# A decoder layer on one core: first output rows transposed ten units later, exps ahead of crossings, pairs 4 to 7 merged on GpSimd

## The chip, the cores and the metric

The kernel runs on one core of one Trainium2 chip. The metric is device time in microseconds (us) of one execution, the median of several runs. Engines: PE is TensorE, PEld its weight loads, DVE VectorE, ACT ScalarE, POOL GpSimd, SP the queue that issues most transfers.

## The reference

One layer for 512 tokens of width 1024, all in float32. One projection `h = x @ w_in` feeds two attention branches of 8 heads each, whose outputs are gated, joined, projected and normalised:

```python
o_a = _dsa_branch(qa, ka, va, iq, ik, iw) * jax.nn.silu(ga)      # A: top-128 keys of an indexer
o_b = _mla_branch(c_q, c_kv, k_rope, ...) * jax.nn.silu(gb)      # B: latent attention, 96-wide q and k
out = jnp.concatenate([o_a, o_b], axis=-1) @ w_out[l]
x = _layernorm(DEEPNORM_ALPHA * x + out, ln_g[l], ln_b[l])
```

Both branches are causal softmax attention, `p = softmax(masked scores * scale)`, `o = p @ v`. Branch A masks all keys but those that its indexer chose.

## The kernel before

**Stages.** Until about 170 us the kernel multiplies x with w_in and makes queries, keys and values. Matrices that need full precision are split into a high and a low part, and a product is three matmuls (high by high, high by low, low by high). Then comes attention, and beside it and behind it the output projection with `w_out` and the layer norm.

**Units.** Attention is a sequence of `NU` = 64 units, one for each (branch, block of 128 query tokens, head). Units 0 to 31 are branch A, units 32 to 63 branch B. The four token tiles come in the order 3, 2, 1, 0, eight heads each, so a unit has 512, 384, 256 and then 128 keys, in each branch. Each engine has its own loop over the unit number u, written out by hand, and semaphores join them:

- PE, iteration u (L1355): `scores(u)`, then the transposes of unit u-2 (`T_LAG`), then the product with v of unit u-4 (`outputs`), then what is put beside: `o_transposes(i, b)` (tile i's gated output rows, half b: 0 for branch A, 1 for B) and some steps of `out_products` (the output projection).
- DVE, iteration u (L992): `mask_unit(u)` adds the mask and finds the maximum, `probs_low(u-2)` (branch B only) makes the low part of the transposed probabilities, and then, in the units that the tables name, the normalising and gating of a tile, `copy_oT_lo`, `gate_obT`, `read_pair`, `merge_pair` and the pieces of the layer norm.
- ACT, iteration u (L665): `copy_probsT(u-2)`, then `copy_oT_hi` and `cross_pair` where due, then `exp_unit(u)`.

The scores of u wait for the mask of u-2, the mask of u for the transposes of u-4, the transposes of u for its exp, the product for the copies.

**PSUM banks of the transposes.** Two banks take all transposes in turn, those of the units and of the output rows. The table `slots` (L82) is their order, and `slot(n)` (L1257) lets a transpose wait until the one two places ahead was read: a unit of branch A by its copy, one of B by `probs_low`, output rows by `copy_oT_lo` or `gate_obT`. `O_FIRST` = 22 puts tile 0's branch A rows behind unit 22's transposes, which PE issues in iteration `O_FIRST + T_LAG` = 24; ACT and DVE read them in their iterations 24.

**Output projection.** The first half of tile 0's 48 steps starts at iteration `A_HALF_AT` = 34, two steps an iteration for 12 iterations. The second half is at iterations 49 to 54, four an iteration, and needs `copy_oT_lo(0, 1)`. From iteration 55 on tile 1 follows with six an iteration.

**Pairs.** In branch B the products of two heads form a pair; pairs 0 to 15, four for each tile. For pair g, DVE's `read_pair(g)` at iteration 38 + 2g sums parts out of PSUM, ACT's `cross_pair(g)` one iteration later moves halves across partitions with two copies, and `merge_pair(g)` adds them with two instructions (L295). Pairs below `POOL_PAIRS` = 8 are merged by DVE in iteration 39 + 2g, behind its own mask and `probs_low`; the rest by POOL in a loop of its own (L468), in which the square roots of the layer norm (`root`) and `scale_gate(2)`, `scale_gate(3)` have fixed places. The second instruction of a pair's merge on POOL waits for nothing on DVE. `gate_obT(i)` waits for all four pairs of tile i.

**Vb.** In ACT's iterations 32 and 33 `vb_high(1)` to `vb_high(3)` (three 512-wide copies, L654) stand behind the exp.

The places that the change and the steps below touch are O_FIRST, A_HALF_AT and POOL_PAIRS (L1395 to L1397), ACT's loop and POOL's loop over pairs.

Of the kernel before, what the change touches and what calls it, by code (L numbers as in the profile page):

```python
# [27 lines left out]
def build(nc, x, xT, positions, freqs, w_in, q_norm_g, w_uq, kv_norm_g, w_ukv, w_out, ln_g, ln_b, out):  # L28
# [40 lines left out]
    NU = 2 * NU_A  # L69
# [3 lines left out]
    def unit(u):  # L73
        v, h = divmod(u, HEADS)
        m = ORDER[v % TT]
        return v, m, h, (m + 1) * P


    O_AFTER = [[NU_A + HEADS * (i + 1) + OT_AT - T_LAG + b for b in range(2)] for i in range(TT - 1)] + [[NU, NU]]
    O_AFTER[0][0] = O_FIRST  # L80
    slots = []
# [109 lines left out]
    with ExitStack() as ctx:  # L191
# [83 lines left out]
        def wait_tok(eng, g, m):  # L275

            eng.wait_ge(acc_read[m], 2 * (g + 1))
# [10 lines left out]
        def merge_pair(eng, g):  # L288

            eng.wait_ge(pair_crossed, 2 * (g + 1))  # L290
            if g % 4 == 0 and g > 0:
                eng.wait_ge(oT_lo_ready, 2 * (g // 4))
            for a in range(2):
                rows = slice(V_DIM * a, V_DIM * (a + 1))
                eng.tensor_tensor(obT[rows, g % 4], half_sum[rows, g % 2, a], crossed[rows, g % 2],  # L295
                                  ALU.add).then_inc(pair_merged, 1)
                if g >= POOL_PAIRS:
                    eng.wait_ge(pair_merged, 2 * g + a + 1)
# [69 lines left out]
        def _(pool):  # L368
# [58 lines left out]
            def scale_gate(i):  # L427

                m = ORDER[i]
                pool.wait_ge(rinv_ready, i + 1)  # L430
                wait_tok(pool, G_GB, m)
                g3 = gate[:, m, A_WIDTH:].rearrange("p (h d) -> p h d", h=HEADS)
                pool.tensor_tensor(g3, g3, rinv.unsqueeze(2).broadcast_to([P, HEADS, V_DIM]), ALU.mult).then_inc(gate_scaled, 1)
# [27 lines left out]
            def root(i):  # L461

                pool.wait_ge(var_ready, i + 1)
                pool.tensor_tensor(rstd, aggr[:, 2:3], minus_half[:, 0:1], ALU.pow).then_inc(rstd_ready, 1)


            scale_gate(1)
            for g in range(POOL_PAIRS, NPAIR):  # L468
                merge_pair(pool, g)
                if g == 9:  # L470
                    root(0)
                if g == 10:
                    scale_gate(2)
                if g == NPAIR - 3:
                    scale_gate(3)
                    root(1)
# [5 lines left out]
        def _(act):  # L482
# [115 lines left out]
            def evac_qpeT(j):  # L598

                quad, r = divmod(j, 2)  # L600
                act.wait_ge(acc_ready, A_END + quad + 1)
                ins = act.activation(qbT[NOPE:B_QK, 4 * quad + r, :], ps_y[32 * r:32 * r + 32, quad], ACT.Copy)
                if r == 1:
                    ins.then_inc(acc_read[2 + quad], 1)


            def exp_unit(u):
                N = unit(u)[3]
                act.wait_ge(masked_ready, u + 1)
                act.activation(probs[:, u % NPROBS, 0:N], probs[:, u % NPROBS, 0:N], ACT.Exp, bias=neg_max[:, u % 8:u % 8 + 1],  # L610
                               scale=-1.0, accum_out=row_sum[:, u:u + 1]).then_inc(probs_ready, 1)
# [12 lines left out]
            def copy_probsT(u):  # L624
                N = unit(u)[3]
                act.wait_ge(transposed, slot_of[u] + 1)
                if u >= 3:
                    act.wait_ge(pv_done, u - 2)
                dst = probsT[:, u % 3, 0:N] if u < NU_A else probsT_b[:, u % 3, 0, 0:N]
                act.activation(dst, ps_pT[:, slot_of[u] % 2, 0:N], ACT.Copy).then_inc(probsT_copied, 1)  # L630

            def copy_oT_hi(i, b):
                n = slot_of[i, b]
                if i == 0 and b == 0:
                    act.wait_ge(wo_hi_ready, 2 * KT)
                if i >= 2 and b == 0:
                    act.wait_ge(out_ps_ready, 2 * (i - 1))
                if b == 0:
                    act.wait_ge(transposed, n + 1)
                    src = ps_pT[:, n % 2].rearrange("p (a b) -> p a b", a=4)  # L640
                else:
                    act.wait_ge(obT_ready, i + 1)
                    src = obT[:, :, :]
                act.activation((oT0, oT1)[i % 2][:, 0, 4 * b:4 * b + 4, :], src, ACT.Copy).then_inc(oT_hi_ready, 1)  # L644

            def vb_high(n):

                j = VB_ORDER[n]
                if n == 1:
                    act.wait_ge(scores_ready, NU_A)  # L650
                    act.wait_ge(masked_ready, NU_A)
                if j == 2:
                    act.wait_ge(vb_lo_dve, 2)
                act.activation(vb_parts[j][:, :, 0:4:3], vb[:, j, :].rearrange("p (q a d) -> p q a d", a=2, d=V_DIM),  # L654
                               ACT.Copy).then_inc(vb_hi_ready, 1)

            def cross_pair(g):

                act.wait_ge(pair_read, g + 1)
                if g >= 2:  # L660
                    act.wait_ge(pair_merged, 2 * (g - 1))
                act.activation(crossed[0:V_DIM, g % 2], half_sum[V_DIM:P, g % 2, 0], ACT.Copy).then_inc(pair_crossed, 1)
                act.activation(crossed[V_DIM:P, g % 2], half_sum[0:V_DIM, g % 2, 1], ACT.Copy).then_inc(pair_crossed, 1)

            for u in range(NU + T_LAG):  # L665
                if u >= T_LAG:
                    copy_probsT(u - T_LAG)
                i, j = divmod(u - NU_A, HEADS)
                if u == O_FIRST + T_LAG:
                    copy_oT_hi(0, 0)  # L670
                if 1 < i < TT and j == OT_AT:
                    copy_oT_hi(i - 1, 0)
                if 0 < i < TT and j == OT_AT + 2:
                    copy_oT_hi(i - 1, 1)
                g = PAIR_AT.get(u - 1)
                if g is not None:
                    cross_pair(g)
                if 2 <= u < NU:
                    exp_unit(u)
                if 0 <= u - PET_AT - 1 < 4:  # L680
                    evac_qpeT(u - PET_AT - 1)
                if u == PET_AT + 7:
                    act.wait_ge(acc_ready, A_END + 3)
                    act.activation(kbT[NOPE:B_QK, 0, :], ps_y[0:ROPE_D, 0], ACT.Copy).then_inc(acc_read[2], 2)
                if u == VB_EARLY:
                    vb_high(0)
                if u == NU_A:
                    vb_high(1)
                    vb_high(2)
                if u == NU_A + 1:  # L690
                    vb_high(3)
# [7 lines left out]
        def _(dve):  # L699
# [160 lines left out]
            def evac_qpeT(j):  # L860

                quad, r = divmod(j, 2)
                dve.wait_ge(acc_ready, A_END + quad + 1)
                ins = V.tensor_copy(qbT[NOPE:B_QK, 4 * quad + 2 + r, :], ps_y[64 + 32 * r:96 + 32 * r, quad])
                if r == 1:
                    ins.then_inc(acc_read[2 + quad], 1)
# [40 lines left out]
            def copy_oT_lo(i, b):  # L907
                dst = (oT0, oT1)[i % 2]
                dve.wait_ge(oT_hi_ready, 2 * i + b + 1)
                src = ps_pT[:, slot_of[i, b] % 2].rearrange("p (a b) -> p a b", a=4) if b == 0 else obT[:, :, :]  # L910
                V.tensor_tensor(dst[:, 1, 4 * b:4 * b + 4, :], src, dst[:, 0, 4 * b:4 * b + 4, :],  # L911
                                ALU.subtract).then_inc(oT_lo_ready, 1)
# [79 lines left out]
            for u in range(NU):  # L992
# [15 lines left out]
                if 0 <= u - PET_AT - 1 < 4:  # L1008
                    evac_qpeT(u - PET_AT - 1)
                if u == O_FIRST + T_LAG:  # L1010
                    copy_oT_lo(0, 0)
# [6 lines left out]
                if u in PAIR_AT:  # L1018
                    read_pair(PAIR_AT[u])
                if u - 1 in PAIR_AT and PAIR_AT[u - 1] < POOL_PAIRS:  # L1020
                    merge_pair(V, PAIR_AT[u - 1])
# [31 lines left out]
        def _(pe):  # L1053
# [301 lines left out]
            for u in range(NU + PV_LAG):  # L1355
# [10 lines left out]
                i, j = divmod(u - NU_A, HEADS)  # L1366
                if u == O_FIRST + T_LAG:
                    o_transposes(0, 0)
                if 0 < i < TT and OT_AT <= j < OT_AT + 2 and (i > 1 or j > OT_AT):
                    o_transposes(i - 1, j - OT_AT)  # L1370
                if 0 <= u - A_HALF_AT < 12:
                    out_products(0, 2 * (u - A_HALF_AT), 2 * (u - A_HALF_AT + 1))
                if 0 <= u - OUT_AT[0] - 2 < 6:
# [18 lines left out]
QT_AT, KT_AT = 4, 4  # L1392
PET_AT = 8
WO_ORDER = (1, 2, 3, 4, 5, 6, 7, 0)
O_FIRST = 22  # L1395
A_HALF_AT = 34
POOL_PAIRS = 8  # L1397
VB_EARLY = 20
Q_ROTATE_AT = [28, 33, 38, 43]

# [38 lines left out]
```

## Time and profile before

| | |
|---|---|
| median of 3 runs | 308.17 us (307.63 to 308.52) |
| profiled execution | 307.56 us |
| its span, first to last instruction | 305.7 us |
| mean granted TensorE clock | 0.993 of full speed |
| PE busy | 293.8 us (96%) |
| DVE, ACT, POOL busy | 236.8, 171.5, 159.8 us |
| chain of work that ended last | 92% on PE |

Times inside the trace count from the first instruction. A matmul's end is modelled and lies a little behind the start of the next one, so a PE delay is best read from starts. In brackets behind a row stands the idle time before it and who ended it.

### The profile page before, as it was taken

The numbers are of one execution on the slowest core, as the hardware profiler recorded it, in microseconds if no ns is written. First come the engines' busy times: TensorE is split into PE (matmuls) and PEld (weight loads), VectorE is DVE, ScalarE is ACT, GpSimd is POOL, SyncE is SP. The second block draws the span as 40 slices with busy tenths as digits, with TensorE's granted clock in tenths as the row PEclk, the third lists the DMA queues.
The fourth block names the chain that finished last, engine by engine and source line by source line (L and its number), as shares of the span: only waits on it lengthen the run. The fifth ranks groups of instructions, "written<-read, shape, count | busy, mean of one in ns | idle before, by whom it ended". The sixth has DMA issues, their size and how long they took to land.

```text
span 305.7 us, 5164 instructions
## 1 busy us (share of the span) xinstructions
PE 293.8 (96%) x1646; PEld 253.2 (83%) x1646; DVE 236.8 (77%) x540; ACT 171.5 (56%) x411; POOL 159.8 (52%) x180
## 2 busy tenths in 40 slices
PE   7999999999999999999999999999999999999990
PEld 6999988888888888888888789997677787888890
DVE  1999968879999999994134645755789998887785
ACT  5844355684152262383277887997967885464200
POOL 4898954305999965435317696820491010335211
PEclk9999999999999999999999999999999999999997
DMA  7974542200533723220068234131940000040411
GB/s 251 343 198 132 151 142 69 69 2 0 146 95 106 207 69 89 85 69 2 0 154 232 99 138 159 49 62 28 360 165 0 2 0 3 0 138 2 137 69 69
DMA packets 14777, 31.24 MB, mean 102 GB/s; under 512 B 1728, under 2 KB 4288, under 8 KB 14752
## 3 DMA queue, kind: packets, MB, share of 16 engines
q1 hardware_dynamic: 14192, 30.60, 32.3%
q10 hardware_dynamic: 560, 0.33, 0.4%
q8 instruction: 13, 0.21, 0.3%
q14 instruction: 12, 0.10, 0.1%
HBM read 26.28 MB, written 2.10 MB: 93 GB/s over the span
## 4 chain that ended last, share of the span: by engine, by line
PE 92%; DVE 2%; DMA 2%; ACT 1%; issue 1%; DVEq 0%; SPq 0%; ACTq 0%
PE ps L1059 49%; PE ps L1348 14%; PE ps L1275 6%; PE ps L1225 5%; PE ps L1291 5%; PE ps L1306 3%; PE ps L1216 2%; DMA x_raw<-in_xT 2%; PE ps L1219 2%; PE ps L1131 1%; PE ps L1069 1%; PE ps L1150 1%; PE ps L1320 1%; PE ps L1121 1%; ACT oT L644 1%
## 5 line engine op out<-in xcount | busy, mean ns | idle before, releaser
L403 POOL TENSOR_TENSOR w_lo<-w_raw,w_hi 128x512 fp32r<-128x512 f32 (+3 forms) x62 | 80.1, 1313 | 37.6 <-ACT w_hi L496 37.6
L1059 PE MATMUL ps<-w_hi,x_lo 128*128 128x512 f32 (+2 forms) x224 | 82.4, 371 | 0.0
L1059 PE MATMUL ps<-w_lo,x_hi 128*128 128x512 f32 (+2 forms) x224 | 82.4, 371 | 0.0
L496 ACT ACTIVATE w_hi<-w_raw 128x512 fp32r<-128x512 f32 (+3 forms) x62 | 36.3, 591 | 73.3 <-PE ps L1059 72.4
L1059 PE MATMUL ps<-w_hi,x_hi 128*128 128x512 f32 (+1 forms) x192 | 74.5, 388 | 0.0
L1059 PEld LDWEIGHTS ps<-w_hi,x_lo 128*128 128x128 f32 x224 | 42.1, 188 | 6.5
L1059 PEld LDWEIGHTS ps<-w_lo,x_hi 128*128 128x128 f32 x224 | 42.1, 188 | 5.8
L1348 PE MATMUL ps<-wo_hi,oT 128*128 128x512 f32 (+1 forms) x144 | 44.3, 372 | 0.0
L610 ACT ACTIVATE probs<-probs,small 128x512 f32<-128x512 f32 (+3 forms) x64 | 35.7, 558 | 10.9 <-DVE small L879 10.5
L1059 PEld LDWEIGHTS ps<-w_hi,x_hi 128*128 128x128 f32 x192 | 36.0, 188 | 5.9
L1275 PE MATMUL ps<-ident,probs 128*128 128x128 f32 x160 | 28.3, 274 | 1.9 <-ACT probs L610 0.9
L1275 PEld LDWEIGHTS ps<-ident,probs 128*128 128x128 f32 x160 | 20.1, 140 | 11.3 <-issue 6.3
L1348 PEld LDWEIGHTS ps<-wo_hi,oT 128*128 128x128 f32 x144 | 25.7, 189 | 3.3
L832 DVE MATCH_REPLACE8 score<-small,score 128x256 f32<-128x256 f32 (+2 forms) x48 | 25.6, 544 | 0.0
L879 DVE CUSTOM_DVE_ANT_0 probs<-ps,score 128x512 f32<-128x512 f32 (+2 forms) x24 | 13.3, 556 | 14.7 <-PE ps L1219 14.7
L829 DVE MAX8 small<-score 128x8 f32<-128x256 f32 (+2 forms) x48 | 23.5, 547 | 0.0
L1225 PE MATMUL ps<-kbT,qbT 96*128 96x512 f32 (+3 forms) x64 | 22.7, 435 | 0.0
L295 POOL TENSOR_TENSOR obT<-half_sum,crossed 64x128 f32<-64x128 f32 x16 | 8.8, 550 | 24.5 <-DVE oT L911 13.7
L1291 PE MATMUL ps<-va,probsT 128*128 128x64 f32 x160 | 21.4, 264 | 0.0
L1291 PEld LDWEIGHTS ps<-va,probsT 128*128 128x128 f32 x160 | 20.6, 193 | 0.6 <-issue 0.6
L879 DVE CUSTOM_DVE_ANT_0 probs<-ps,causal 128x128 f32<-128x128 f32 (+3 forms) x40 | 17.6, 444 | 3.5 <-PE ps L1225 1.6
L630 ACT ACTIVATE probsT_b<-ps 128x512 fp32r<-128x512 f32 (+3 forms) x32 | 13.8, 431 | 8.2 <-PE ps L1275 8.1
(164 smaller groups left out, 565.0 us busy)
## 6 DMA issues: line engine op xcount, KB each, us to landing
w_raw<-in_w_in SPq DMA_DIRECT2D x20, 512.0 KB, 3.6
kaT_swap<-kaT SPq DMA_DIRECT2D x8, 256.0 KB, 3.7
w_raw<-in_w_out SPq DMA_DIRECT2D x4, 512.0 KB, 5.1
wo_early<-in_w_out SPq DMA_DIRECT2D x4, 512.0 KB, 4.1
wo_raw_b<-in_w_out SPq DMA_DIRECT2D x4, 512.0 KB, 5.4
x_res<-in_x SPq DMA_DIRECT2D x4, 512.0 KB, 7.0
w_raw<-in_w_in SPq DMA_DIRECT2D x4, 416.0 KB, 3.9
x_raw<-in_xT SPq DMA_DIRECT2D x3, 512.0 KB, 6.4
```

The source lines that it names most:

```text
L403: pool.tensor_tensor(w_lo[:, s, 0:n], w_raw[:, s, 0:n], w_hi[:, s, 0:n], ALU.subtract).then_inc(w_lo_ready, 1)
L496: act.activation(dst, w_raw[:, s, 0:n], ACT.Copy).then_inc(w_hi_ready, 1)
L610: act.activation(probs[:, u % NPROBS, 0:N], probs[:, u % NPROBS, 0:N], ACT.Exp, bias=neg_max[:, u % 8:u % 8 + 1], scale=-1.0, accum_out=ro ...
L630: act.activation(dst, ps_pT[:, slot_of[u] % 2, 0:N], ACT.Copy).then_inc(probsT_copied, 1)
L829: step(V.max(top8[:, 8 * j:8 * j + 8], sc))
L832: step(V.match_replace(out=sc, in_to_replace=top8[:, 8 * j:8 * j + 8], in_values=sc, imm_value=TAKEN))
L879: V.tensor_tensor_reduce(out=probs[:, u % NPROBS, 0:N], in0=ps_s[:, u % 2, 0:N], in1=bias, scale=-scale, scalar=3.0e38, op0=ALU.add, op1=A ...
L1059: ins = mm(dst, a, b, start=start and j == 0, stop=stop and j == len(pairs) - 1)
L1225: ins = mm(ps_s[:, b, 0:N], qbT[:, h, t], kbT[:, h, 0:N], start=True, stop=True)
L1275: ins = nc.tensor.transpose(bank[:, j * P:(j + 1) * P], probs[:, u % NPROBS, j * P:(j + 1) * P], ident[:, :])
L1291: ins = mm(ps_o[:, v % 2, h * A_DIM:(h + 1) * A_DIM], probsT[:, u % 3, j * P:(j + 1) * P], va[:, j, h * A_DIM:(h + 1) * A_DIM], start=(j = ...
L1348: ins = mm(out_ps(i, b), oT[i % 2][:, o, k, :], w[:, wcols], start=(r == 0), stop=(r == 3 * KT - 1))
```

## The change

Five numbers and places change. Tile 0's branch A output rows are transposed ten units later (iteration 34, behind unit 32's transposes), and the first half of its output projection starts at iteration 36. DVE merges pairs 0 to 3 only, POOL 4 to 15, and `scale_gate(1)` moves behind two of POOL's new merges. In ACT's iteration the exp comes ahead of `copy_oT_hi(i - 1, 1)` and of `cross_pair`, but stays behind `copy_probsT` and behind `copy_oT_hi(.., 0)`. All of the work stays the same.

```diff
-            scale_gate(1)
             for g in range(POOL_PAIRS, NPAIR):
+                if g == POOL_PAIRS + 2:
+                    scale_gate(1)
                 merge_pair(pool, g)
...
                     copy_oT_hi(0, 0)
                 if 1 < i < TT and j == OT_AT:
                     copy_oT_hi(i - 1, 0)
+                if 2 <= u < NU:
+                    exp_unit(u)
                 if 0 < i < TT and j == OT_AT + 2:
                     copy_oT_hi(i - 1, 1)
                 g = PAIR_AT.get(u - 1)
                 if g is not None:
                     cross_pair(g)
-                if 2 <= u < NU:
-                    exp_unit(u)
...
-O_FIRST = 22
-A_HALF_AT = 34
-POOL_PAIRS = 8
+O_FIRST = 32
+A_HALF_AT = 36
+POOL_PAIRS = 4
```

ACT, iterations 39 and 40 of before (copy, crossing of pair 0, exp, then copy and exp):

```order
L630 ACTIVATE probsT_b_92<-ps 128x512 [waits pv_done,transposed]
L662 ACTIVATE crossed_110<-half_sum_103 64x128 [waits pair_read]
L663 ACTIVATE crossed_110<-half_sum_103 64x128
L610 ACTIVATE probs_97,small_107<-probs_97,small_107 128x512 [waits masked_ready]
L630 ACTIVATE probsT_b_92<-ps 128x512 [waits pv_done,transposed]
L610 ACTIVATE probs_97,small_107<-probs_97,small_107 128x384 [waits masked_ready]
```

The same iterations of the changed kernel, whose lines count one more:

```order
L631 ACTIVATE probsT_b_92<-ps 128x512 [waits pv_done,transposed]
L611 ACTIVATE probs_97,small_107<-probs_97,small_107 128x512 [waits masked_ready]
L663 ACTIVATE crossed_110<-half_sum_103 64x128 [waits pair_read]
L664 ACTIVATE crossed_110<-half_sum_103 64x128
L631 ACTIVATE probsT_b_92<-ps 128x512 [waits pv_done,transposed]
L611 ACTIVATE probs_97,small_107<-probs_97,small_107 128x384 [waits masked_ready]
```

The crossing now stands behind an instruction that waits for DVE's mask of the same unit.

ACT, iterations 33 to 35 of the changed kernel, with the copy of tile 0's output rows (oT_66) between unit 32's copy and unit 34's exp:

```order
L631 ACTIVATE probsT<-ps 128x128 [waits pv_done,transposed]
L611 ACTIVATE probs,small<-probs,small 128x512 [waits masked_ready]
L655 ACTIVATE vb_parts_95<-vb 128x4x2x64 [waits vb_lo_dve]
L631 ACTIVATE probsT_b<-ps 128x512 [waits pv_done,transposed]
L645 ACTIVATE oT_66<-ps 128x512 [waits transposed,wo_hi_ready]
L611 ACTIVATE probs,small<-probs,small 128x512 [waits masked_ready]
L631 ACTIVATE probsT_b<-ps 128x512 [waits pv_done,transposed]
```

Before, that copy stood ahead of unit 24's exp. The copy of unit 32 is the first of branch B, and it is behind the last of the vb copies in both kernels.

## Rows read from the trace of the kernel before

**Rows 1.** The page: the span, and the chain that ended last, by engine.

```profile
span 305.7 us, 5164 instructions
...
PE 92%; DVE 2%; DMA 2%; ACT 1%; issue 1%; DVEq 0%; SPq 0%; ACTq 0%
```

**Rows 2.** Timeline, PE and PEld, iterations 24 to 26: start, length, engine, line, what.

```profile
206.32 0.61 PE L1320 MATMUL ps<-ident,gate 128*128 128x128 f32 x4
206.68 0.31 PE L1216 MATMUL ps<-kaT,qaT 128*128 128x128 f32 x1
...
208.40 0.14 PEld L1275 LDWEIGHTS ps<-ident,probs 128*128 128x128 f32 x1 [0.58 <-DVE oT L911]
```

**Rows 3.** Timeline, iterations 34 and 35: PE, then ACT's and DVE's copies of unit 32.

```profile
214.95 1.08 PE L1225 MATMUL ps<-kbT,qbT 96*128 96x512 f32 x2
215.86 0.60 PE L1275 MATMUL ps<-ident,probs 128*128 128x128 f32 x4
...
216.44 0.48 PE L1348 MATMUL ps<-wo_hi,oT 128*128 128x512 f32 x1
...
217.64 0.58 ACT L630 ACTIVATE probsT_b<-ps 128x512 fp32r<-128x512 f32 x1
...
218.25 0.69 DVE L919 TENSOR_TENSOR probsT_b<-ps,probsT_b 128x512 fp32r<-128x512 f32 x1 [0.58 <-ACT probsT_b L630]
```

**Rows 4.** Timeline, iterations 39 to 47: masks, exp, crossing and transposes.

```profile
226.79 0.68 DVE L879 CUSTOM_DVE_ANT_0 probs<-ps,causal 128x512 f32<-128x512 f32 x1
...
233.40 0.56 DVE L879 CUSTOM_DVE_ANT_0 probs<-ps,causal 128x384 f32<-128x384 f32 x1
...
234.00 0.62 ACT L610 ACTIVATE probs<-probs,small 128x384 f32<-128x384 f32 x1 [0.35 <-DVE small L879]
...
235.01 0.55 DVE L879 CUSTOM_DVE_ANT_0 probs<-ps,causal 128x384 f32<-128x384 f32 x1
...
239.31 0.31 ACT L662 ACTIVATE crossed<-half_sum 64x128 f32<-64x128 f32 x1
...
240.62 0.56 DVE L879 CUSTOM_DVE_ANT_0 probs<-ps,causal 128x384 f32<-128x384 f32 x1
...
241.72 0.36 PEld L1275 LDWEIGHTS ps<-ident,probs 128*128 128x128 f32 x3 [0.35 <-DVE probsT_b L919]
```

**Rows 5.** Timeline, PE, iteration 49: scores of unit 49, transposes of unit 47.

```profile
243.63 0.60 PE L1225 MATMUL ps<-kbT,qbT 96*128 96x256 f32 x2
244.90 0.52 PE L1275 MATMUL ps<-ident,probs 128*128 128x128 f32 x3 [0.68 <-ACT probs L610]
```

**Rows 6.** Timeline, iterations 53 and 55: DVE's merge of pair 7, and PE.

```profile
255.03 0.60 DVE L295 TENSOR_TENSOR obT<-half_sum,crossed 64x128 f32<-64x128 f32 x2
...
256.72 0.60 PE L1225 MATMUL ps<-kbT,qbT 96*128 96x256 f32 x2
257.81 0.44 PE L1275 MATMUL ps<-ident,probs 128*128 128x128 f32 x2 [0.49 <-DVE probsT_b L919]
```

**Rows 7.** Timeline, iterations 55 to 60, by engine: DVE, ACT, POOL and PE.

```profile
258.87 0.41 DVE L879 CUSTOM_DVE_ANT_0 probs<-ps,causal 128x256 f32<-128x256 f32 x1
259.54 0.68 DVE L911 TENSOR_TENSOR oT<-obT,oT 128x512 fp32r<-128x512 f32 x1
...
262.84 0.31 ACT L662 ACTIVATE crossed<-half_sum 64x128 f32<-64x128 f32 x1
263.89 0.40 ACT L610 ACTIVATE probs<-probs,small 128x128 f32<-128x128 f32 x1 [0.41 <-DVE small L879]
...
263.63 1.54 POOL L295 TENSOR_TENSOR obT<-half_sum,crossed 64x128 f32<-64x128 f32 x2 [2.26 <-ACT crossed L663]
268.49 1.00 POOL L295 TENSOR_TENSOR obT<-half_sum,crossed 64x128 f32<-64x128 f32 x2 [2.69 <-ACT crossed L663]
...
266.90 0.40 ACT L610 ACTIVATE probs<-probs,small 128x128 f32<-128x128 f32 x1 [2.22 <-DVE small L879]
...
268.00 0.27 PE L1275 MATMUL ps<-ident,probs 128*128 128x128 f32 x1
```

## The prediction

> **What bounds the kernel now.** First the page: the chain that ended last lies 92% on PE, of a span of 305.7 us [rows 1]. So only two things move the end: PE's work, which this change leaves as it is, and the moments in which PE waits. I then looked at who PE waits for and at the timeline of the 64 attention units. From unit 56 on PE runs without a gap until it is done, so a wait saved or added among the units goes to the end one for one. In branch B and the end of branch A there are three waits that the change aims at.
>
> - Iteration 26: 0.58 us [rows 2] until DVE has read the output rows out of the bank that unit 24's transposes need; by starts it is 0.60.
> - Iteration 49: the scores of a 256-key unit take 0.45 (half of the 0.91 between the two starts of the 512-key unit in [rows 3]). The transposes could start at 243.63 + 0.45 = 244.08 and start at 244.90 [rows 5]: 0.82, for unit 47's exp, which stands behind the output copy and the crossing on ACT.
> - Iteration 55: 256.72 + 0.45 = 257.17 against 257.81 [rows 6]: 0.64, for DVE's `probs_low`, which is late.
>
> Together 2.06 us. A fourth, around iterations 30 and 31, comes from normalising and gating on DVE and stays.
>
> **The change part by part.** I go along PE's time and call "shift" how much later than before an iteration starts, with work that was moved counted where it now stands.
>
> *Output rows out of iteration 24.* The four transposes take 206.68 - 206.32 = 0.36 [rows 2], the wait 0.60. Iteration 34 starts 0.96 early, at 213.99 instead of 214.95 [rows 3]. ACT and DVE there are chained to PE and move along.
>
> *Output rows into iteration 34.* The new slot order is 32, rows, 33, 34. So unit 33's transposes take the bank of unit 32 and need `probs_low(32)`, which before only unit 34's needed, an iteration later. ACT reaches unit 32's copy behind three vb copies: 217.64 before, now 216.68. `probs_low(32)` starts 0.61 later [rows 3], at 217.29, and releases PE at its end, 0.69 + 0.06 later: 218.04. And PE? Scores 0.91 and then 0.58 up to the place where the projection steps stood (216.44 - 215.86) bring it to 215.48; a short wait of 0.06 for unit 31's copy, the rows' transposes 0.36, and iteration 35 starts at 215.90, its scores end at 216.81. It has no projection steps any more (two of them took 0.55 in each of iterations 34 and 35, the distance from 216.44 to the next scores). **PE waits 1.23 us in iteration 35.** Shift after it: -0.96 + 0.36 + 0.06 + 0.05 + 1.23 - 2 x 0.55 = about -0.37. The four steps come back in iterations 46 and 47.
>
> ACT's copy of the rows and DVE's `copy_oT_lo(0, 0)` fit: 0.6 each, while PE stands.
>
> *Exp ahead of the crossing, while DVE still merges.* This is the step to watch. In iteration 39 + 2g DVE runs mask, `probs_low`, merge; the merge waits for the crossing, and the crossing now waits for the exp, which waits for the mask that DVE has just made. The round for a 384-key unit: mask to exp 234.00 - 233.40 = 0.60, exp 0.62, crossing's start to the mask behind the merge 240.62 - 239.31 = 1.31 [rows 4]. So 2.53 us from an odd mask to the next, with DVE idle for part of it. The even iteration takes 235.01 - 233.40 = 1.61 [rows 4]. A pair of units costs DVE 4.14 us. The masks of before, which kept PE's pace, took 240.62 - 226.79 = 13.83 for seven units, of which a good part was the first, longest ones and a merge that took 1.5 us; units 43 to 46 went at 3.7 a pair. DVE becomes the pace. From mask 39 at 226.79 - 0.37 = 226.42: iteration 39, 512 keys, 2.94 (0.1 more for the mask, 0.1 for the exp and 0.2 for unit 37's copy ahead of it); then 1.6, 2.5, 1.6, 2.5, 1.6, 2.5, in all 12.4, for masks 40 to 46: mask 46 at about 241.79 instead of 240.62. From that mask to the weight load of unit 45's transposes it took 241.72 - 240.62 = 1.10, and there the load waited for `probs_low` already [rows 4]: no slack was left. Now it loads at 242.89. PE took these transposes 0.11 behind the load, at 241.83; now it is 0.37 early but has two projection steps more in iteration 46, 0.46, and would be there at 241.92. **PE waits 1.0 us in iteration 47.**
>
> *Iteration 49.* The 0.82 is gone: exp 47 now starts 0.60 behind its mask. But the output copy `copy_oT_hi(0, 1)` is behind it, 0.62 later, and the projection's second half needs `copy_oT_lo(0, 1)` in iteration 49. Mask 47 comes 2.16 behind mask 46 (`probs_low`, gate and `read_pair` lie between), at 243.95; + 0.60 + 0.62 + 0.65 for exp and high part, + 0.73 for the low part: ready at 246.55. PE, freed at 242.92, has 3.4 us of matmuls to do until then, 246.33: **0.2 us.**
>
> *Merges 4 to 7 off DVE.* 0.60 each [rows 6]. Three of them were hidden; pair 7's stood ahead of the layer norm pieces and mask 54, and without it `probs_low(52)` is in time: the 0.64 of iteration 55 is gone. On POOL, mostly idle there, a pair takes 1.00 [rows 7]; `gate_obT(1)` needs pair 7 some 0.5 us after it is ready. `scale_gate(1)`, 1.0 behind pair 5, has ten units of room. Each costs nothing.
>
> *Iterations 55 to 60.* A chain ran here with 0.46 to spare: exp 58 started at 266.90, its transposes can follow 0.64 later, and PE took them at 268.00 [rows 7]. Exp 58 waits for mask 58, that for `ln_scale(0, 0)`, that for POOL's `root(0)`, that for pair 9's merge and so for its crossing. In the frame of before: PE is 0.64 earlier, and so is DVE's chain (0.60 to 0.64, the merge). Added are: `copy_oT_hi(1, 1)` behind exp 55, which starts 0.45 behind mask 55 at 258.87 and takes 0.51, so the low part starts at 258.87 + 0.45 + 0.51 + 0.65 = 260.48 instead of 259.54, +0.94 [rows 7]; the crossing of pair 9 behind exp 57, at 263.89 + 0.40 = 264.29 instead of 262.84, +1.45; and pair 9's merge takes 1.00 instead of 1.54, if nothing disturbs it, -0.54. In sum +1.85 on a slack of 0.46: **PE waits 1.4 us in iteration 60** (1.35 with the smaller roundings). Later places have over 1 us in hand.
>
> The sum: 1.23 + 1.0 + 0.2 + 1.35 = 3.8 added, 2.06 removed, **+1.7 us**. Against the profiled execution's 307.56 that is 309.3. The three runs have a median of 308.17, 0.6 above it; I put the sum on the median: 309.9.
>
> **A rule that bears on it.** Pair 9's merge on POOL took 1.54 us, others 1.00 [rows 7], and DVE ran a layer norm piece with two SBUF inputs beside it. The Trainium skill (SBUF — State Buffer, "Who interferes with whom") says that a DVE instruction with two SBUF inputs and a GpSimd instruction that reads SBUF lock each other out for a whole instruction. By that rule, the trace agrees, and more merges on POOL are more chances for it. As a mechanism here: if the merge of pair 9 meets `ln_centre` again it takes 1.54, not 1.00, the wait in iteration 60 is 1.9 and the sum +2.2: 310.4. I take 1.00, since in my timeline `ln_centre` is over when the crossing ends.
>
> **Rivals.**
>
> - *Faster: DVE does not fall behind.* One mechanism: the round over ACT is hidden, because the first units of the stretch are long and DVE has more in hand than I count. Then there is no wait in iteration 47 and none in 60, and what is left is 1.2 - 2.06 = -0.8: 307.3; should unit 32's copy come in time too, -2.1: 306.1. It decides at mask 46: before 240.9 there is no loss. For it speaks that DVE is idle in part of each odd iteration; against it that the load behind mask 46 had no slack before.
> - *About the same.* Only one of the two late waits is there in full; for example the layer norm chain fits because crossing 9 is not held up: 1.23 + 1.0 + 0.2 - 2.06 = +0.4: 308.5.
> - *The lock* above: 310.4.
> - *The change is not what it says:* "ahead of its copies" does not hold for `copy_probsT`, which still precedes the exp. If the exp did gain on unit copies, nothing above would change, since exps of units 34 to 46 are paced by masks.
>
> **How the numbers follow.** A measurement of this kernel tells a change from none at about 0.3%, 0.9 us. My forecast 309.9 gets 0.48, the lock 0.10, the middle case 0.24, the faster rival 0.18. Slower by over 0.3% is the first two, 0.58; same 0.24; faster 0.18. The unknown parts are the three waits, each the small difference of two long chains, good to 0.4 us each. The range takes the middle case, the near end of the faster one and the lock with 0.6 on top: 307.2 to 311.0.
>
> **What would show it.** No wait before unit 24 to 27's transposes; a wait of over 1 us before unit 33's transposes, ended by DVE's `probs_low`; DVE's merges of pairs 0 to 3 each with some 0.8 us of idle time before them, ended by ACT's crossing; a wait before unit 45's transposes; none before 53's; pair 9's crossing behind exp 57 and a wait before unit 58's transposes, ended by ACT's exp. I am wrong if masks 40 to 46 keep PE's pace, or if PE's waits in the units together are no longer than before.

## The result, and the profile after

The changed kernel takes **311.63 us** (median of 4 runs, 311.33 to 311.75) against 307.93 for the kernel before on the same chip; the ratio is 1.0116, 95% interval 1.0098 to 1.0135. It is 3.7 us slower. Slower was right, but I had said 309.9 and at most 311.0: less than half of the loss was in my sum. The profiled execution took 311.70, with a span of 309.9 against 305.7 [rows 1]. Executions of one and the same kernel can come out some 1.7 us apart by what happens in their first 15 us (of `p_best` below: 306.01 to 306.64 and 307.80 to 308.17), so small differences between the kernels below are read from waits and distances and not from medians.

The page after: the span, and the chain that ended last, which lies less on PE and more on DVE and ACT.

```profile
span 309.9 us, 5166 instructions
...
PE 85%; DVE 5%; issue 3%; ACT 2%; DMA 2%; POOL 0%; SPq 0%; DVEq 0%; ACTq 0%; POOLq 0%
```

The waits of PE after, by who ended them: line and what it waited for, then us in total, times, longest. The first line below is the start of the program, the others are attention and the steps behind it.

```profile
PE ps L1070 <- ACT w_hi L497: 2.3, 3, 1.2
PE ps L1276 <- DVE probsT_b L920: 1.9, 2, 1.0
...
PE ps L1226 <- DVE small L880: 0.9, 1, 0.9
PE ps L1321 <- DVE probsT_b L920: 0.5, 1, 0.5
PE ps L1349 <- issue: 0.3, 1, 0.3
```

Where PE stands, from its timeline (start, length, engine, line, what, idle time before it and who ended it):

```profile
218.35 0.66 PE L1276 MATMUL ps<-ident,probs 128*128 128x128 f32 x4 [1.00 <-DVE probsT_b L920]
...
240.39 0.60 PE L1307 MATMUL ps<-probsT_b,vb_parts 128*128 128x256 f32 x3
241.10 0.66 PE L1321 MATMUL ps<-ident,gate 128*128 128x128 f32 x4
...
243.74 0.55 PE L1276 MATMUL ps<-ident,probs 128*128 128x128 f32 x3 [0.88 <-DVE probsT_b L920]
...
247.45 0.47 PE L1349 MATMUL ps<-wo_hi,oT 128*128 128x512 f32 x1
...
270.12 0.49 PE L1226 MATMUL ps<-kbT,qbT 96*128 96x128 f32 x2 [0.93 <-DVE small L880]
270.74 0.30 PE L1276 MATMUL ps<-ident,probs 128*128 128x128 f32 x1
...
273.68 0.66 PE L1321 MATMUL ps<-ident,gate 128*128 128x128 f32 x4 [0.47 <-DVE probsT_b L920]
...
291.38 0.47 PE L1349 MATMUL ps<-wo_hi,oT 128*128 128x512 f32 x1 [0.31 <-issue]
```

By distances between starts, each against the same pair of instructions where nothing waits, these cost:

| place | forecast | measured |
|---|---|---|
| iteration 35, transposes of unit 33 | 1.23 | 1.18 |
| iteration 46, tile 0's branch B rows | none | **0.27** |
| iteration 47, transposes of unit 45 | 1.0 | 1.05 |
| iteration 49, projection's second half | 0.2 | 0.3 |
| iteration 60, scores of 60 and transposes of 58 | 1.35 | 1.08 + 0.40 |
| iteration 61, tile 2's branch A rows | none | **0.63** |
| first projection step of tile 3 | none | **0.44** |
| iterations 26, 49 and 55 of before, gone | -2.06 | -2.06 |

For iteration 46 the pair is the product and the rows' transposes: 241.10 - 240.39 = 0.71 against 0.44 in the kernel before. The measured terms make 5.35 - 2.06 = 3.3. From the start of iteration 24 to PE's last matmul it takes 302.57 - 205.82 = 96.75 us instead of 298.35 - 205.43 = 92.92, so 3.83 more. The other 0.5 lies right behind the waits, where the next matmuls follow more slowly: the whole stretches that hold the waits of iterations 46, 47, 60, 61 and of tile 3 are 0.32, 1.10, 1.73, 0.68 and 0.57 us longer than in `a_noexp` below, which has none of these waits, and so each 0.05 to 0.25 longer than the wait in it. The last 0.4 of the span's 4.2 lies ahead of iteration 24 (205.82 against 205.43), where the two kernels do the same; other executions differ there too. I use this **distance** for the experiments, since it leaves the start out.

DVE's round in the stretch of pairs 1 to 3, from DVE's timeline: mask 43, merge, mask 44, mask 45, merge, mask 46.

```profile
235.84 0.55 DVE L880 CUSTOM_DVE_ANT_0 probs<-ps,causal 128x384 f32<-128x384 f32 x1
...
237.84 0.60 DVE L295 TENSOR_TENSOR obT<-half_sum,crossed 64x128 f32<-64x128 f32 x2 [0.97 <-ACT crossed L664]
238.47 0.56 DVE L880 CUSTOM_DVE_ANT_0 probs<-ps,causal 128x384 f32<-128x384 f32 x1
...
240.02 0.55 DVE L880 CUSTOM_DVE_ANT_0 probs<-ps,causal 128x384 f32<-128x384 f32 x1
...
242.02 0.60 DVE L295 TENSOR_TENSOR obT<-half_sum,crossed 64x128 f32<-64x128 f32 x2 [0.97 <-ACT crossed L664]
242.65 0.56 DVE L880 CUSTOM_DVE_ANT_0 probs<-ps,causal 128x384 f32<-128x384 f32 x1
```

An odd round takes 238.47 - 235.84 = 2.63, an even one 240.02 - 238.47 = 1.55. DVE stands idle for 0.97 us with the next mask ready to be made (PE had started the scores of 44 at 235.90), because a merge is ahead of it in its queue. ACT's part of the same round, exp 43 and the crossing of pair 2:

```profile
236.43 0.62 ACT L611 ACTIVATE probs<-probs,small 128x384 f32<-128x384 f32 x1 [0.52 <-DVE small L880]
236.95 0.19 ACT L611 ACTIVATION_READ_ACCUMULATOR probs<-probs,small 128x1 f32 x1
237.16 0.31 ACT L663 ACTIVATE crossed<-half_sum 64x128 f32<-64x128 f32 x1
```

### The profile page after: what moved, and what is told of

It reads as the page before. It is cut to its first block, busy times and chain, and to the rows that moved or that the text cites. A ratio compares the mean times of both kernels' runs of the same rounds, so it can differ in the third digit from the quotient of the medians.

```text
span 309.9 us, 5166 instructions
## 1 busy us (share of the span) xinstructions
PE 295.4 (95%) x1646; PEld 253.0 (82%) x1646; DVE 232.5 (75%) x532; ACT 171.8 (55%) x411; POOL 162.9 (53%) x188
## 4 chain that ended last, share of the span: by engine, by line
PE 85%; DVE 5%; issue 3%; ACT 2%; DMA 2%; POOL 0%; SPq 0%; DVEq 0%; ACTq 0%; POOLq 0%
PE ps L1060 49%; PE ps L1349 12%; PE ps L1292 5%; PE ps L1276 5%; PE ps L1226 3%; PE ps L1217 2%; DMA w_raw<-in_w_in 2%; PE ps L1307 2%; PE ps L1220 2%; PE ps L1132 1%; DVE probsT_b L920 1%; PE ps L1070 1%; PE ps L1151 1%; PE ps L1321 1%; PE ps L1122 1%
## 5 line engine op out<-in xcount | busy, mean ns | idle before, releaser
L295 POOL TENSOR_TENSOR obT<-half_sum,crossed 64x128 f32<-64x128 f32 x24 | 11.8, 494 | 38.3 <-DVE oT L912 18.7
L920 DVE TENSOR_TENSOR probsT_b<-ps,probsT_b 128x512 fp32r<-128x512 f32 (+3 forms) x32 | 15.6, 486 | 4.4 <-ACT probsT_b L631 4.2
```

Source lines behind the costliest of these rows:

```text
L920: V.tensor_tensor(probsT_b[:, w, 1, 0:N], ps_pT[:, slot_of[u] % 2, 0:N], probsT_b[:, w, 0, 0:N], ALU.subtract).then_inc(probsT_lo_ready, 1)
```

## The experiments

My theory **R** was that the exp-first order (the exp ahead of the output copy and the crossing) costs the time at two separate places: while DVE merges, through the round mask, exp, crossing, merge; and from unit 55 on, through a chain on ACT, GpSimd and DVE. Against it stood **M** (the moved output rows cost the most), **P** (merges on GpSimd come late) and **E** (exp-first costs by itself, whoever merges). Spans and distances are of one profiled execution each; the kernel before has 305.7 and 92.92.

### One part alone, and all but one

`b_exp` is the kernel before with the exp moved ahead, and nothing else:

```diff
+                if 2 <= u < NU:
+                    exp_unit(u)
                 if 0 < i < TT and j == OT_AT + 2:
                     copy_oT_hi(i - 1, 1)
...
                     cross_pair(g)
-                if 2 <= u < NU:
-                    exp_unit(u)
```

> The kernel before with the exp moved ahead of the output copy and the crossing, alone. Theory R (round): DVE merges pairs 0 to 7 here, each merge behind a crossing that is behind an exp that waits for DVE's own mask, so DVE loses some 0.8 us in each odd unit from 39 to 53; PE waits over 1 us in iterations 46 or 47 and again in iterations 55 to 60. The 0.6 of iteration 26 stays. At least +2.5 us on before (over 310.4). Theory M (the moved rows cost the time, the exp order helps as it says): the 0.8 of iteration 49 goes and nothing comes, 307.1. Theory P (merges on GpSimd are late): no merge is moved here, so 307.1 as well.

Measured: **314.8 us**, ratio 1.0225 (1.0194 to 1.0256), span 312.9, distance 99.97. This part alone costs 6.7 us, more than the whole change. PE's waits:

```profile
PE ps L1275 <- DVE probsT_b L919: 2.3, 2, 1.3
...
PE ps L1320 <- DVE probsT_b L919: 1.4, 3, 0.7
...
PE ps L1225 <- DVE small L879: 0.9, 1, 0.9
```

The round now goes on through pair 7, and it holds up output rows too (L1320, three times).

`b_rows` is the kernel before with the rows and the first half of the projection moved:

```diff
-O_FIRST = 22
-A_HALF_AT = 34
+O_FIRST = 32
+A_HALF_AT = 36
```

> The kernel before with O_FIRST = 32 and A_HALF_AT = 36, alone. All theories have the wait of iteration 26 gone (-0.6) and one before unit 33's transposes (+1.2). The two projection steps in each of iterations 46 and 47 also cover the wait of iteration 49 (-0.8). Theory R: -0.2, no difference that can be measured, 307.7. Theory M: the moved rows are the main loss, +2 us or more, 310.

Measured: 308.01 us, ratio 0.9998 (0.9977 to 1.0019), distance 93.07, +0.15. The wait in iteration 35 is there (1.16), those in 49 (0.39) and 55 (0.65) too, and that of iteration 26 is gone. M falls: the move gives and takes about the same.

`b_pool` is the kernel before with pairs 4 to 7 on GpSimd:

```diff
-            scale_gate(1)
             for g in range(POOL_PAIRS, NPAIR):
+                if g == 6:
+                    scale_gate(1)
...
-POOL_PAIRS = 8
+POOL_PAIRS = 4
```

> The kernel before with POOL_PAIRS = 4 and scale_gate(1) moved, alone. Theory R: only the 0.65 of iteration 55 goes, 307.3, and DVE's layer norm pieces come about 0.6 earlier. Theory P: pairs merged on GpSimd take 1.0 instead of 0.6 and hold up gate_obT or the root, so 309 or more, with a wait of DVE on GpSimd around iterations 47 to 57.

Measured: 307.3 us, ratio 0.998 (0.9958 to 1.0003), span 305.2, distance 92.22, -0.70. The wait of iteration 55 is gone, nothing comes in its place. P falls.

`a_noexp` is the changed kernel with ACT's old order, so the last two parts together.

```diff
-                if 2 <= u < NU:
-                    exp_unit(u)
                 if 0 < i < TT and j == OT_AT + 2:
...
                     cross_pair(g)
+                if 2 <= u < NU:
+                    exp_unit(u)
```

> The changed kernel with ACT's order of before (crossing and output copy ahead of the exp). Theory R: of the waits added by the change only that before unit 33's transposes is left (1.2), and all three old ones are gone (2.1): 307.0, some 4.6 us under the changed kernel. Theory M: the loss stays, about 311. Theory P: about 310.5, since only the 1.0 of iteration 47 goes.

Measured: **307.47 us**, ratio 0.997 (0.9951 to 0.9989), span 305.4, distance 92.36. Of the waits only iteration 35 (1.17) and iteration 49 (0.38) are left; I had expected the latter to be gone too. So the exp-first order costs the changed kernel 311.63 - 307.47 = 4.2 us, 4.39 by distance, and the rest of the change gains 0.3%.

### Is it the round over DVE?

`a_pool0` is the changed kernel with all pairs merged on GpSimd, so that no merge stands in DVE's queue:

```diff
-POOL_PAIRS = 4
+POOL_PAIRS = 0
...
-                if g == POOL_PAIRS + 2:
+                if g == 2:
+                    scale_gate(0)
+                if g == 6:
                     scale_gate(1)
```

> The changed kernel with all 16 pairs merged on GpSimd (scale_gate(0) then goes behind pair 1, scale_gate(1) behind pair 5), exp still ahead of the crossing. Theory R (the loss of iterations 46 and 47 is the round mask, exp, crossing, merge on DVE): with no merge on DVE the masks keep PE's pace and the 1.4 us of waits in iterations 46 and 47 go; those of 60 and 61 stay: 310.2. Theory E (the exp ahead of the crossing costs by itself, whoever merges): 311.6, with the waits of 46 and 47 still there.

Measured: 310.05 us, ratio 1.0061 (1.0039 to 1.0083), span 308.3, distance 95.01. The waits of iterations 46, 47 and 49 are gone, and DVE's masks wait for PE again, as in this timeline of DVE (masks 44 and 46):

```profile
236.83 0.56 DVE L880 CUSTOM_DVE_ANT_0 probs<-ps,causal 128x384 f32<-128x384 f32 x1 [0.51 <-PE ps L1226]
...
240.42 0.56 DVE L880 CUSTOM_DVE_ANT_0 probs<-ps,causal 128x384 f32<-128x384 f32 x1 [0.38 <-PE ps L1226]
```

The exp-first order is still there, so E falls for this stretch. The waits of iterations 60 and 61 and of tile 3's first step stay.

### Are the two places independent?

`a_early` has exp first only in units 2 to 46, `a_late` only from unit 47 on (and the old place otherwise):

```diff
-                if 2 <= u < NU:
+                if 2 <= u < NU and (u < 47):
                     exp_unit(u)
...
                     cross_pair(g)
+                if 2 <= u < NU and not (u < 47):
+                    exp_unit(u)
```

> The changed kernel with the exp moved ahead only in units 2 to 46, the order of before from 47 on. Theory R: the waits of iterations 46 and 47 (1.4) stay and may add 0.3 in iteration 49, those of 60 and 61 (2.1, and 0.4 at the start of the last tile's steps) go: 309.2, 2.4 under the changed kernel. If the late waits were a consequence of DVE's early lag, they would be there still: 311.6.

Measured: 308.48 us, ratio 1.0027 (1.0004 to 1.0049), span 306.5: waits in iterations 35, 46 (0.28), 47 (1.04) and 49 (0.38), none in 60 or 61.

> The changed kernel with the exp moved ahead only from unit 47 on. Theory R, with two places that don't depend on each other: no waits in 46 and 47, 2.1 us in iterations 60 and 61 and 0.4 later: 309.9, 1.7 under the changed kernel. If the late waits came from the early lag: 307.3.

Measured: 311.03 us (median of 4, the profiled one 309.76 with span 308.0), ratio 1.0088 (1.0061 to 1.0116): waits in iterations 35, 60 (1.13 + 0.40), 61 (0.63) and before tile 3's first step (0.3 by the waits view), none in 46 or 47. The distance is 92.36 us in `a_noexp`, 93.80 in `a_early` (+1.44), 94.94 in `a_late` (+2.58) and 96.75 in the changed kernel (+4.39). The two make 4.02; the other 0.37 is iteration 49, where `a_late` saves the 0.38 and the changed kernel spends it again on the low part (0.3). Otherwise the places are independent; the late one, of which I had named one wait of three, is the larger.

### What makes up the late loss?

Three kernels with ACT's old order in all units but the named ones. Baseline is `a_noexp` with its distance of 92.36. The diff is that of the first.

```diff
-                if 2 <= u < NU:
+                if 2 <= u < NU and (u == 57):
                     exp_unit(u)
...
                     cross_pair(g)
+                if 2 <= u < NU and not (u == 57):
+                    exp_unit(u)
```

> The changed kernel with ACT's old order in all units but 57, where exp 57 stands ahead of the crossing of pair 9. Theory R (PE's wait in iteration 60 is the sum of two delays: the crossing of pair 9 behind exp 57, and tile 1's last output copy behind exp 55): only the first is there, 1.45 later less the 0.54 by which the merge on GpSimd is shorter, on a slack of about 0.5, so a wait of 0.3 to 0.6 us in iteration 60, 307.8 us. Rival S (the crossing of pair 9 alone is the cause): the whole wait of 1.1 + 0.4 us in iteration 60, and with it the 0.6 in iteration 61; 309.5 us. Both: waits of 1.2 in iteration 35 and 0.4 in iteration 49 stay.

Measured: 308.82 us, ratio 1.0015 (0.999 to 1.004), span 306.3, distance 93.16, +0.80. The scores of 60, usually 0.23 behind the last step, start 0.38 behind it, and the transposes of 58 another 0.62 later instead of 0.22. By starts PE waits 0.15 + 0.40 = 0.55, within R's 0.3 to 0.6; S had 1.5:

```profile
267.35 0.39 PE L1351 MATMUL ps<-wo_hi,oT 128*128 128x512 f32 x1
267.73 0.49 PE L1228 MATMUL ps<-kbT,qbT 96*128 96x128 f32 x2
268.35 0.30 PE L1278 MATMUL ps<-ident,probs 128*128 128x128 f32 x1
```

`l_555` has it in units 55 and 57 (`u in (55, 57)`):

> As the last one, but exp ahead in units 55 and 57. Theory R: both delays are there, so the full 1.1 + 0.4 us in iteration 60, and as a consequence of exp 58 being late also the 0.6 in iteration 61 and the 0.4 ahead of tile 3's steps; 309.5 us or a little more. Rival S: no more than with unit 57 alone. Third, T (the waits of iteration 61 and of tile 3 have a cause of their own, exp 59 ahead of the crossing of pair 10): they are missing here, 308.9 us.

Measured: 308.99 us, ratio 1.0025 (1.0006 to 1.0045), span 307.1, distance 94.04, +1.68.

```profile
267.29 0.39 PE L1351 MATMUL ps<-wo_hi,oT 128*128 128x512 f32 x1
268.61 0.49 PE L1228 MATMUL ps<-kbT,qbT 96*128 96x128 f32 x2 [0.93 <-DVE small L882]
```

So unit 55, through tile 1's output copy, adds 0.88, close to the 0.94 of my step. R holds for iteration 60, and S falls. But the waits of iteration 61 and of tile 3 are not here: they do not follow from a late exp 58, as I had expected of this run. T takes their place.

`l_59` has it in unit 59 alone:

> As the last ones, but exp ahead in unit 59 alone. Theory R: no wait in iterations 60 and 61, nothing ahead of tile 3, 307.5 us, as with ACT's old order throughout. Rival T: the wait of 0.6 in iteration 61 is there without the one in iteration 60; 308.1 us.

Measured: 307.71 us, ratio 0.9994 (0.9973 to 1.0015), distance 92.79, +0.43; nothing in iteration 60, and the wait of iteration 61 by itself, 0.40 by starts (ACT and DVE first, then PE):

```profile
270.75 0.31 ACT L664 ACTIVATE crossed<-half_sum 64x128 f32<-64x128 f32 x1
271.08 0.28 ACT L631 ACTIVATE probsT_b<-ps 128x128 fp32r<-128x128 f32 x1
...
271.39 0.29 DVE L922 TENSOR_TENSOR probsT_b<-ps,probsT_b 128x128 fp32r<-128x128 f32 x1 [1.12 <-ACT probsT_b L631]
...
271.11 0.27 PE L1278 MATMUL ps<-ident,probs 128*128 128x128 f32 x1
...
271.74 0.66 PE L1323 MATMUL ps<-ident,gate 128*128 128x128 f32 x4 [0.23 <-DVE probsT_b L922]
```

T holds there, but not for tile 3, before whose first step this run has no wait. In the order `slots` tile 2's branch A rows come behind unit 59, so their bank is that of unit 58. It is freed by `probs_low(58)`, which waits for ACT's copy of unit 58 (271.08), and that now stands behind exp 59 and the crossing of pair 10. With the old order ACT makes this crossing while it waits for mask 59.

What is left is the 0.44 before tile 3's first step. No run had exp 63 ahead alone, so the cause of this one is not shown by a run; I only read it from the traces. ACT's copy of tile 2's branch B rows is behind exp 63; changed kernel, ACT, then DVE's low part:

```profile
278.91 0.40 ACT L611 ACTIVATE probs<-probs,small 128x128 f32<-128x128 f32 x1 [0.26 <-DVE small L880]
...
279.31 0.61 ACT L645 ACTIVATE oT<-obT 128x512 fp32r<-128x512 f32 x1
...
279.96 0.69 DVE L912 TENSOR_TENSOR oT<-obT,oT 128x512 fp32r<-128x512 f32 x1 [0.88 <-ACT oT L645]
...
290.59 0.69 DVE L912 TENSOR_TENSOR oT<-ps,oT 128x512 fp32r<-128x512 f32 x1 [1.33 <-ACT oT L645]
```

From the one low part to the other DVE takes 290.59 - 279.96 = 10.63, and with the old order too (285.92 - 275.29): it is the pace there. PE's transposes of tile 3's rows moved by 287.31 - 283.37 = 3.94 between the two kernels, this chain of DVE by 4.67. It is 0.73 later for PE, which had about 0.3 in hand.

### Two versions with the old order

`p_o34`: what does the wait of iteration 35 hang on, and does it go if the rows stand behind unit 34? Against `a_noexp` it has:

```diff
-O_FIRST = 32
-A_HALF_AT = 36
+O_FIRST = 34
+A_HALF_AT = 37
```

> ACT's order of before, POOL_PAIRS = 4, O_FIRST = 34, A_HALF_AT = 37: the output rows two units later than in the changed kernel, behind the time in which ACT is held up by the vb copies. Theory R with the wait of 1.2 before unit 33's transposes put down to those copies: that wait shrinks to 0.3 or nothing, the three old waits are gone: 306.2 to 306.5, under both kernels and 1.0 under the changed kernel with ACT's old order. If the wait is a matter of the slot order alone (a unit's transposes needing the unit just before), it is there again in iteration 37, 1 us or more: 307.3.

Measured: 307.67 us, ratio 0.9984 (0.9963 to 1.0005), span 304.8, distance 91.89. The wait of 1.17 is gone, and so is that of iteration 49, since two projection steps now stand in iteration 48 ahead of it; 0.50 comes back in iteration 37, whose projection steps wait for the low part of the rows, behind a normalising on DVE (221.49 is `copy_oT_lo(0, 0)`):

```profile
220.88 0.69 DVE L897 TENSOR_TENSOR o_norm<-ps,small 128x512 f32<-128x512 f32 x1
221.49 0.68 DVE L912 TENSOR_TENSOR oT<-ps,oT 128x512 fp32r<-128x512 f32 x1
```

`p_best` gives that low part one iteration more, and takes exp first in unit 47 alone, whose exp iteration 49 waited for in the old order. Against the changed kernel:

```diff
-                if 2 <= u < NU:
+                if 2 <= u < NU and (u == 47):
                     exp_unit(u)
...
                     cross_pair(g)
+                if 2 <= u < NU and not (u == 47):
+                    exp_unit(u)
...
-O_FIRST = 32
-A_HALF_AT = 36
+O_FIRST = 34
+A_HALF_AT = 38
```

> ACT's old order but for unit 47, pairs 4 to 15 on GpSimd, tile 0's first output rows behind unit 34's transposes (O_FIRST = 34), its projection from iteration 38 (A_HALF_AT = 38). Theory: the wait before unit 33's transposes is away as with O_FIRST = 34 before, the 0.5 in iteration 37 too, since the low part of the rows has one more iteration, and the 0.4 in iteration 49 goes back to 0.2 since exp 47 comes 0.6 earlier but the output copy later. 307.0 us, below both kernels. Rival: the steps that moved to iterations 48 and 49 find a wait of their own, 307.6 us.

Measured: **306.41 us**, ratio 0.9952 (0.9935 to 0.997). It is below both kernels. Of PE's waits in attention 0.2 us is left, in branch A:

```profile
PE ps L1278 <- ACT probs L611: 0.2, 1, 0.2
```

The distance is 91.34, 1.58 less than in the kernel before and 5.41 less than in the changed one. Of the 0.55 by which it is below `p_o34`, 0.50 is the wait of iteration 37; what exp 47 ahead is worth by itself in this kernel, no run shows.

## Why the prediction was half right

**What bounds the kernel: right.** Waits of PE among the units went to the end in full: the table's 3.3 us are found again in the distance of 3.8, with the 0.5 right behind the waits.

**Output rows out of iteration 24 and into 34: right.** Forecast 1.23, measured 1.18, ended by `probs_low(32)`. `b_rows` shows that the move by itself changes nothing (my terms for it: 1.23 + 0.2 at most, less 0.60 and part of the 0.82). `p_o34` shows that it is the place behind unit 32 that costs; that its copy is late because of the vb copies ahead of it is read from ACT's queue, and no run moved them.

**The round over ACT: right in place and price, but not in its reach.** Forecast 2.53 for an odd round, measured 2.63: from the start of the exp to that of the crossing it takes 0.73 and not 0.62. The idle times of 0.67 to 0.97 us before the merges, the wait of 1.05 in iteration 47 and its cure in `a_pool0` are as the step said. That 1.05 stands beside a forecast of 1.0 is partly luck, though: in the frame of before (0.39 less) mask 46 came at 242.26 and not at 241.79, 0.47 late, and PE itself came 0.4 late to the same place, three quarters of it by the wait of iteration 46. **The first failed step is here:** I followed the late masks to one reader, unit 45's transposes. The output rows of iteration 46 take the bank that `probs_low(43)` frees, and that stands in the same late queue: 0.27 us, which `a_pool0` removes together with the other.

**Iteration 49: right,** 0.3 for 0.2.

**Merges 4 to 7 on GpSimd: right,** they cost nothing and the wait of iteration 55 is gone.

**Iteration 60: right.** 1.35 forecast, 1.48 measured. `l_57` and `l_555` measured its two parts, 0.80 and 0.88, in sum 1.68 with the slack already taken off; I had 1.45 - 0.54 and 0.94 on a slack of 0.46, which makes 1.39. The difference is that here PE waits twice, and that the sign I named was the smaller one: the scores of 60 wait 1.08 for mask 58, and only then the transposes of 58 another 0.40 for exp 58.

**"Later places have over 1 us in hand": wrong, and this is the main failed step.** I put one sentence where a count was due. The same two moves come back there: the crossing of pair 10 behind exp 59 holds up the copy of unit 58 (0.63 in iteration 61; `l_59` shows 0.40 of it alone), and the copy of tile 2's branch B rows behind exp 63 goes with 0.44 at tile 3 (by the traces only). Together 1.07 us, 1.25 with what lies right behind them, all of it absent from the sum.

In all: 0.27 + 1.07 from places not looked at, 0.2 from terms a little small, 0.4 from the start of the execution and 0.5 right behind the waits. With 1.7 forecast that is 4.1, the difference of the profiled executions (311.70 and 307.56).

**The rivals.** DVE did fall behind, so the faster case is out. The middle case is out: both late waits are there. The lock did not meet pair 9's merge, which took 0.98:

```profile
267.39 0.98 POOL L295 TENSOR_TENSOR obT<-half_sum,crossed 64x128 f32<-64x128 f32 x2 [3.81 <-ACT crossed L664]
```

Elsewhere it can be seen: in `p_o34` a product on DVE takes 1.66 while GpSimd makes the low parts of w_out (L457, from 221.89 on for 4.20), and 1.14 in the changed kernel, where the same product elsewhere takes 0.69. In the kernel before it starts at 223.96, just ahead of one of GpSimd's instructions (224.02): there it takes 0.68, and GpSimd's takes 1.77 where the median of the eight is 1.28.

```profile
223.29 1.66 DVE L906 TENSOR_TENSOR gate<-o_norm,gate 128x512 f32<-128x512 f32 x1
```

The Trainium skill (SBUF — State Buffer, "Who interferes with whom") lets two such instructions shut each other out; these rows agree, but neither holds up PE.

**The range** was too narrow since it held only the errors of waits that I had found, and nothing for those that I had not.

## What to carry to other kernels

When an instruction is put ahead of another in one engine's queue, list every place in the program where the pair comes up, and at each one all readers of what is now late, the buffers' next users among them: of the 4.39 us that the swap cost here, 1.25 lay behind the last place that was worked out. An order that closes a ring over two in-order queues (mask, exp, crossing, merge, next mask) can set the pace even if both engines are idle for part of each round, as here; taking one member out of the ring cured it. And a swap can take away a wait in one iteration (49) and bring others elsewhere, so it pays to test it by unit.

## What the runs showed of the hardware

- Exp to copy on ACT takes 0.62 from start to start, but exp to crossing 0.73: the read of the exp's accumulator (0.19, from 236.95) is over before the crossing starts, while a copy of the transposes starts beside it, and so does the output copy (245.39 to 246.00, 0.61). Why the two differ, no run here tells.
- PE's granted clock can fall near the start of an execution. In `p_best`'s profiled execution PE had idled for 1.80 us up to 8.85, and the granted clock was at the lower level, 1.2 GHz, between 10 and 13 us; iteration 24 then starts at 207.54. In the kernel before PE had idled for 1.19, the clock stayed at 2.4 GHz, and iteration 24 starts at 205.43. Stretches of `p_best` (PE, PEld, DVE, ACT and POOL busy, then PEclk, DMA share and GB/s):

```profile
9.00:10.00 1.00, 1.00 (x7) 1.00 (x8) 0.78 (x2) 0.92 (x3) 1.00 (x2) 0.84 1.05 373
10.00:11.00 1.00, 1.00 (x5) 1.00 (x5) 1.00 (x2) 0.75 (x3) 1.00 (x1) 0.50 1.05 375
```

The clock fell likewise in the profiled executions of `b_rows` (behind 1.81 us of idle time) and `l_59` (behind 1.55), but not in that of `a_pool0` (behind 1.56). So the length of this gap alone does not decide it, and what does, no run here tells.
